# Spread stage of a streaming encoder layer: token index innermost in both matmul operands

## The reference, cut to what matters

```python
expert = jnp.take_along_axis(cand_i, best_pos, axis=-1)      # expert = 128 * i + j
gate = jax.nn.softmax(best_s, axis=-1)
a = jnp.einsum('td,thkd->thk', hb, expert_u[expert]).astype(jnp.float32)
act = (jax.nn.gelu(a, approximate=False) * gate).astype(hb.dtype)
return jnp.einsum('thk,thkd->td', act, expert_v[expert])
```

## Time and profile before

| | |
|---|---|
| median of 3 runs | 3873.57 us |
| the profiled execution's own time | 3871.7 us |
| its span, first to last instruction | 3869.9 us |
| mean granted TensorE clock | 0.955 of full speed |
| spread stage, first `hot_j` to the issue of the last store | 1580.6 to 1837.1 us |
| last store of the stage, from its issue to the next stage's first work | 1837.1 to 1868.3 us |
| experts stage | 1868.3 us to the end |

### The profile page before, as it was taken

The page is one execution under the profiler, slowest core; times in us unless marked ns, Lnnn a source line. Parts: engine busy times, 40 slices in busy tenths (PEclk is TensorE's granted clock), DMA queues, the critical chain, the costliest instruction groups (busy, mean ns, idle before and its releaser), DMA issues.

```text
span 3869.9 us, 49782 instructions
## 1 busy us (share of the span) xinstructions
PE 3343.5 (86%) x17534; PEld 2831.2 (73%) x17534; DVE 2667.2 (69%) x5420; ACT 1084.9 (28%) x1628; POOL 1622.4 (42%) x1283
## 2 busy tenths in 40 slices
PE   7999996999979981466299998998999999999999
PEld 6888874566539871465288887888888888888888
DVE  3000004444324999899288998998988899899998
ACT  3111112333311110599122222222222222222221
POOL 0000005323100000000367777777777687777775
PEclk9999997999989995799599999999999999999999
DMA  3222215222222000155988998999988899999997
GB/s 134 93 92 92 92 60 214 93 96 77 91 89 95 16 5 7 41 161 159 328 307 309 334 329 314 335 330 332 336 312 323 316 347 353 337 358 348 343 347 278
DMA packets 338429, 833.98 MB, mean 216 GB/s; under 512 B 25856, under 2 KB 128640, under 8 KB 337024
## 3 DMA queue, kind: packets, MB, share of 16 engines
q0 software_dynamic: 129024, 469.82, 33.1%
q1 hardware_dynamic: 180768, 323.26, 24.8%
q10 hardware_dynamic: 28512, 39.52, 2.8%
HBM read 743.71 MB, written 88.80 MB: 215 GB/s over the span
## 4 chain that ended last, share of the span: by engine, by line
PE 23%; DVE 15%; POOL 7%; issue 5%; DMA 1%; ACT 0%; ACTq 0%; DVEq 0%; SPq 0%
PE exp_vp L1870 12%; PE exp_up L1853 11%; DVE exp_ring L1788 5%; DVE exp_now L1795 4%; POOL exp_ring L1618 4%; DVE exp_acc L1766 3%; DVE exp_am_lo L1757 2%; POOL exp_v_lo L1609 2%; POOL exp_u_lo L1604 1%; DMA exp_u_raw<-in_u 1%; DVE exp_pr L1752 1%; DMA exp_acc<-scratch_h2T 0%; ACT exp_am_hi L1673 0%; DVE exp_now L1791 0%; DVE exp_dot L1788 0%
## 5 line engine op out<-in xcount | busy, mean ns | idle before, releaser
L1853 PE MATMUL exp_up<-exp_h_hi,exp_u_hi 128*128 128x320 f32 x2048 | 637.5, 311 | 54.9 <-POOL exp_u_lo L1604 54.9
L1618 POOL DMA_INDIRECT exp_ring<-in_u_rows,exp_eid x448 | 425.1, 949 | 565.7 <-DMA exp_eid<-scratch_eid 300.8
L1870 PE MATMUL exp_vp<-exp_v_hi,exp_am_hi 128*128 128x512 f32 x1280 | 515.0, 402 | 145.3 <-POOL exp_v_lo L1609 65.9
L1853 PE MATMUL exp_up<-exp_h_lo,exp_u_hi 128*128 128x320 f32 x2048 | 637.8, 311 | 0.0
L1853 PE MATMUL exp_up<-exp_h_hi,exp_u_lo 128*128 128x320 f32 x2048 | 637.7, 311 | 0.0
L1795 DVE SCALAR_TENSOR_TENSOR exp_now<-exp_ring,exp_dot,exp_now 128x1024 f32<-128x1024 f32 x444 | 569.9, 1284 | 15.9 <-DVE exp_now L1795 0.9
L1766 DVE TENSOR_TENSOR exp_acc<-exp_acc,exp_vp 128x512 f32<-128x512 f32 x640 | 435.5, 681 | 169.0 <-PE exp_vp L1870 155.5
L1788 DVE CUSTOM_DVE_ANT_0 exp_ring<-exp_now,exp_ring 128x1024 f32<-128x1024 f32 x448 | 533.5, 1213 | 1.0 <-ACT exp_now L1730 1.0
L1618 POOL DMA_INDIRECT exp_ring<-in_v,exp_eid x448 | 424.5, 948 | 217.6 <-DVE exp_now L1795 112.5
L1870 PE MATMUL exp_vp<-exp_v_hi,exp_am_lo 128*128 128x512 f32 x1280 | 510.2, 399 | 0.0
L1870 PE MATMUL exp_vp<-exp_v_lo,exp_am_hi 128*128 128x512 f32 x1280 | 505.1, 395 | 0.0
(11 more groups left out here) (202 smaller groups left out, 5267.1 us busy)
## 6 DMA issues: line engine op xcount, KB each, us to landing
exp_u_raw<-in_u SPq DMA_DIRECT2D x128, 512.0 KB
exp_v_raw<-in_v SPq DMA_DIRECT2D x128, 512.0 KB
scratch_gates<-spr_g SPq DMA_DIRECT2D x5, 8192.0 KB
exp_gt<-scratch_gates SPq DMA_DIRECT2D x128, 320.0 KB
scratch_z<-prj_zo ACTq DMA_DIRECT2D x33, 768.0 KB, 3.5
prj_w_raw<-in_w_in SPq DMA_DIRECT2D x44, 512.0 KB, 4.2
mix_zg<-scratch_z SPq DMA_DIRECT2D x9, 1024.0 KB
rt_wq<-in_w_q SPq DMA_DIRECT2D x4, 2048.0 KB, 15.0
```

The costliest lines, as they stand in the source:

```text
L1618: nc.gpsimd.indirect_dma_start(out=ring[:, n % RING, :], out_offset=None, in_=d["u_rows"] if n < PICKS else d["v"], in_offset=bass.Indirec ...
L1853: last = nc.tensor.matmul(up[:, g, 0:GW], u[a][:, o, k * P:(k + 1) * P], h2[b][:, k, cols(g)], start=(k == 0 and n == 0), stop=(k == KD - ...
L1870: last = nc.tensor.matmul(vp[:, bank, :], am[b][:, 1 - half, o, t * P:t * P + P], v[a][:, 2 * (1 - half) + o, c], start=(o == 0 and n == 0 ...
```

## The change

`rows` and `cols` are laid out like `hot_i` and `hot_j`: [entry, number, 8 tokens]. ScalarE and VectorE then read and write every operand in order, and the swap moves to the matmuls: for token b they read `rows[:, :, b]` and `cols[:, :, b]`, 128 f32 elements each 8 elements (32 bytes) apart. The numbers of instructions, the shapes, the waits and the values are the same.

```diff
-        rows = s.sb("rows", [P, 2, B, P])
-        cols = s.sb("cols", [P, 2, B, P])
+        rows = s.sb("rows", [P, 2, P, B])
+        cols = s.sb("cols", [P, 2, P, B])
...
-                    nc.vector.tensor_tensor(cols[:, q % 2, :, :], hot_j[:, q % 2, :, :].rearrange("p k b -> p b k"),
-                                            rt[:, 2, at(tok, B)].rearrange("p (b o) -> p b o", o=1).broadcast_to([P, B, P]),
+                    nc.vector.tensor_tensor(cols[:, q % 2, :, :], hot_j[:, q % 2, :, :],
+                                            rt[:, 2, at(tok, B)].rearrange("p (o b) -> p o b", o=1).broadcast_to([P, P, B]),
                                             ALU.mult).then_inc(cols_ready, 1)
...
-                        last = nc.tensor.matmul(gp[:, q % BANKS, b * P:(b + 1) * P], rows[:, q % 2, b, :], cols[:, q % 2, b, :],
+                        last = nc.tensor.matmul(gp[:, q % BANKS, b * P:(b + 1) * P], rows[:, q % 2, :, b], cols[:, q % 2, :, b],
                                                 start=True, stop=True)
...
-                    nc.scalar.copy(rows[:, q % 2, :, :], hot_i[:, q % 2, :, :].rearrange("p k b -> p b k")).then_inc(rows_ready, 1)
+                    nc.scalar.copy(rows[:, q % 2, :, :], hot_i[:, q % 2, :, :]).then_inc(rows_ready, 1)
```

## The result

The changed kernel takes **3938.4 us** (median of 4 runs, 3936.68 to 3944.42) against 3875.7 us (4 runs). The ratio is 1.0165, 95% interval 1.0147 to 1.0183: slower by 62.7 us. The forecast was 3940.5. Each ratio in this text is against executions of the kernel before that ran beside the changed one, so its time differs a little from one experiment to the next (3872 to 3877 us).

A forecast was written before the change was run, and what follows sets the result against it. VectorE was taken to bound the kernel at 3.11 us a step; TensorE would take over at 3.87, issuing the last store 66.9 us later, which added to 3873.6 gave 3940.5 us. Range 3800 to 3962, own range 3919 to 3958.

The forecast's parts named there:

- The parts removed: Spread stage: cols on VectorE falls from 2014 to 1222 ns, the cast to rows on ScalarE from 2051 to 1042.
- The price of the strided read: TensorE's matmul operands, read 32 bytes apart: 1.81 ns an element, taken over from cols and rows on the other engines.
- Middle case: TensorE reads each strided element once at 1.81 ns: 0.242 us a record, 3.87 us a step, 3940.5 us; chance 0.42.
- The strided cast of the earlier trace: In route, 128 elements 64 bytes apart take 259 ns: 0.84 ns an element, less than a weight load's 0.95.
- the lowest end: TensorE's strided reads add nothing, as 0.84 ns an element is less than the 0.95 a weight load has.
- rival 1: TensorE reads strided at no cost, VectorE bounds at 2.34 us a step: 62 us less, 3811.6 us; chance 0.34.
- each element is fetched once: TensorE's f32 record runs over its columns twice but reads each strided element once: 128 x 1.81 = 232 ns.
- rival 2: TensorE fetches again for the second run, or load and matmul share a path: 0.47 us a record, 4231 us; chance 0.14.
- The bound moved: Spread stage: TensorE becomes the bound at 3.87 us a step, above VectorE's 2.34 and ScalarE's 2.05.
- The sum: Spread stage: 1583.2 start, 309.8 of steps, 8.8 where tiles meet, 1 and 1.1: last store issued at 1903.9, 66.9 us later.
- the term for the first matmuls at the lower clock: Start of the spread stage on TensorE: 1 us added because the first matmuls run at the lower clock.
- a need of 3.05 us a step: ScalarE before the change: 2.04 + 1.01 us of work a step, 0.06 us behind VectorE, the bound.

The follow-up runs named there:

- Experiments 1 to 6: Spread-stage variants of the changed kernel: one operand strided alone, elements 8, 16, 12 or 64 bytes apart, fp32r or bf16 operands; 3805.0 to 3937.2 us.
- e9_bf16_moving: Changed kernel with rows and cols in bf16, rows swapped by ScalarE and read in order, cols at a stride of eight bf16 (16 bytes): 3854.0 us.
- e1_moving: Changed kernel with rows back to ScalarE's swapped copy and read in order; only the moving operand cols keeps the stride of eight: 3936.2 us, ratio 1.0156.
- e2_weights: Changed kernel with cols back to VectorE's swapped product and read in order; only the stationary operand rows keeps the stride of eight: 3937.2 us, ratio 1.0158.
- e3_pairs: Changed kernel with rows and cols grouped by two tokens instead of eight, so matmuls read f32 elements 8 bytes apart: 3815.8 us, ratio 0.9847.
- e5_f32r_moving: Changed kernel with both operands in fp32r, rows swapped by ScalarE and read in order, cols at the stride of eight: 3855.4 us.
- e6_f32r_pairs: Changed kernel with rows and cols in fp32r and grouped by two tokens instead of eight: 3811.6 us.

## Why the prediction was right

- **The parts removed** were right to a few ns: `cols` 1225 (1222 forecast), the cast 1048 (1042). The rows in order of other stages priced them.
- **The price of the strided read** was the choice that mattered. Middle case: 0.242 us a record; measured: 0.240. It carried over from VectorE and ScalarE to TensorE because it is a price of the 16 bytes and not of an engine. Experiments 1 to 6 bear this out: at 4 and 8 bytes next to nothing is paid, at 12 three quarters, at 16 and 32 all of it, by either operand, and at either clock of TensorE. The strided cast of the earlier trace rows, 0.84 ns an element (0.83 by its own sum), on which the lowest end and rival 1 stood, was no guide for TensorE. Why that cast is so quick no run tells.
- **That each element is fetched once** was taken and not shown. e9_bf16_moving shows it, together with the f32 records at the lower clock. That load and matmul don't add up, e1_moving and e2_weights show. With both, rival 2 is gone. For the Trainium skill's two independent read ports (TensorE: Matmul & The Clock Gate, Part 2) this is agreement: 0.233 and 0.238 us alone, 0.240 together.
- **The bound moved** as said: TensorE has 2.23 us of waiting where tiles meet (2.2 forecast), none inside a tile, and a tile is 63.9 us (1646.31 to 1710.21 for two issues of the store; 64.1 forecast).
- **The sum**: the last store was issued at 1901.6 us, forecast 1903.9. 1.4 of the 2.3 us are the pitch: five tiles of 61.67 us make 308.4, forecast 309.8. The other 1.0 is the term for the first matmuls at the lower clock, and that term was wrong. The clock was 0.50 up to 1589.8 us, and yet the first tile takes 61.67 us like the three behind it, as strided records keep their 0.240 us at either clock. (The start, 1583.4 against 1583.2, gives 0.2 back.) The stage grew by 64.5 us and the medians by 62.7, where 66.9 were forecast. That 3940.5 lies only 2.1 us from 3938.4 is in part luck: the kernel before took 3875.7 us beside the changed one and not the 3873.6 that I had added to.
- **Rival 1's time** of 3811.6 us was the right price for the removed part: e3_pairs, in which next to nothing is paid for the reads, takes 3815.8.
- **One term was mis-sized without effect.** I gave ScalarE a need of 3.05 us a step before, by adding two durations. In e5_f32r_moving, where nothing else is slower, its copy and its swapped cast follow each other every 2.89 us with durations of 1.1 and 2.16: ScalarE's records overlap like VectorE's. So ScalarE needs 2.89 us at most, and VectorE bounded the kernel before by some 0.2 us a step, not by 0.06.
- **Rule beside measurement.** The Trainium skill's rule (SBUF — State Buffer, Specifications: 16-byte lines, two hits for full bandwidth) pointed in the right direction. TensorE agrees with it: records 0.125 us apart at 8 bytes (two hits), 0.175 at 12, 0.236 at 16 and 0.240 at 32, where each operand also pays alone. It gives no price, and the 64-byte run is a tenth off what one fixed price would make.

## What to carry to other kernels

Moving a transposed access from one engine to another moves its price with it: here every f32 or bf16 element that is alone in its 16 bytes costs 1.7 to 1.9 ns (a record's distance divided by 128). VectorE and ScalarE paid it side by side for 1024 elements a step each. TensorE has two records for each f32 product, so it pays for 2048 in a row. Look for a layout that shares the stride: two tokens innermost instead of one or eight give each side two elements in 16 bytes, and 58 us are gained where the full swap lost 63. Ask first which engine has room: TensorE had 1.2 us in a step of 3.11, and the swap asked for 1.9 more.

## What the runs showed of the hardware that I had not expected

- A strided f32 record takes the same time at both clock levels of TensorE (0.239 and 0.240 us), an in-order one 0.214 and 0.121. So the slower clock of the first microseconds costs the changed kernel nothing.
- With products in fp32r or bf16 TensorE's clock stayed at the lower level for the whole stage (0.50 granted), with f32 products it rose within the first tile. The stage didn't get slower by it, as other engines set its step. Why it stayed low no run tells; in e6_f32r_pairs TensorE was busy 82% of the window at 0.50, in the kernel before 68% at 0.95.
- At the lower clock an fp32r record of 128 columns follows the last one in 0.213 us inside a step, as long as an f32 record, of which a product has two; bf16 needs 0.107. In e5_f32r_moving, at the same clock, fp32r records of 320 columns (L1853) start 0.267 us apart. So fp32r with 128 columns costs twice as much for each column as with 320.
- ScalarE's copy out of PSUM (L1475) reads elements 512 bytes apart and takes 1.01 us for 1024, no more than a cast in order (1042 ns). So that read of PSUM shows no such price.
- Elements 64 bytes apart are read faster (0.217 us a record) than 32 bytes apart (0.240).
- Writing pairs of f32 with a gap of 4 bytes costs VectorE nothing (1226 against 1225 ns) and ScalarE a few ns beside the same reads without the gap (1155 against 1141).
- Reading pairs of bf16 costs ScalarE a tenth (1141 against 1048 ns) and VectorE nothing (1219 against 1225).
